# A hybrid decoder layer on one core: y of three head groups turned by VectorE and a round trip through memory instead of by TensorE

## The reference

```python
hn = rms_norm(h, norm_mix_w)
u, z, xbc, dt = split(hn @ w_in)                   # 512 | 1536 | 2560 | 24
y_pool = pool_mixer(u, pool_w, pool_scale)
xbc = silu(causal_dwconv(xbc, conv_w, conv_b))     # x 1536 | B 4x128 | C 4x128
y = ssd_chunked(x, softplus(dt + dt_bias), a, B, C) + d_skip * x   # 4 groups of 6 heads, chunks of 128
y = y * silu(z)
y = y * rsqrt(mean(y * y) + EPS) * ssm_norm_w      # mean over the 384 channels of a group
h = h + concat(y_pool, y) @ w_out
h = h + relu(rms_norm(h, norm_ffn_w) @ w_ff1) ** 2 @ w_ff2
out = rms_norm(h, norm_f_w)[:, N_META:]
```

## Time and profile before

| | us |
|---|---|
| median of 3 runs | 2657.96 (2656.44 to 2659.02) |
| profiled execution, its own time | 2655.4 |
| its span | 2653.7 |
| mixer steps of block 1 | from 452 to 652 |
| TensorE busy | 2630.8 (99% of the span) |

### The profile page before, as it was taken

One profiled execution on the slowest core, in us unless ns is written; L12 is line 12 of the kernel. 1 busy time (PEld: TensorE's weight loads), 2 busy tenths in 40 slices (PEclk: granted clock), 3 DMA queues, 4 the chain that ended last, 5 costly groups with the idle time before them and its releaser, 6 DMA issues.

```text
span 2653.7 us, 37407 instructions
## 1 busy us (share of the span) xinstructions
PE 2630.8 (99%) x13818; PEld 2199.1 (83%) x13818; DVE 1674.7 (63%) x2264; ACT 1241.4 (47%) x2474; POOL 1110.9 (42%) x866
## 2 busy tenths in 40 slices
PE   8999999999999999999999999999999999999998
PEld 6888788888888888888888888888888888888887
DVE  6788715888157882478853576564445766666667
ACT  4667653666236662356724455554544222222223
POOL 2133440345004450034544688665555435353434
PEclk9999999999999999999999999999999999999999
DMA  9977676886548866579773655764446742423324
GB/s 333 306 258 244 236 250 247 242 244 220 215 184 264 245 193 235 198 228 253 215 273 138 212 203 198 265 246 142 164 138 236 282 152 101 159 96 127 119 95 159
DMA packets 372739, 551.58 MB, mean 208 GB/s; under 512 B 139450, under 2 KB 240830, under 8 KB 364494
## 3 DMA queue, kind: packets, MB, share of 16 engines
q1 hardware_dynamic: 353550, 539.75, 60.1%
q10 hardware_dynamic: 19008, 9.44, 1.2%
HBM read 393.75 MB, written 155.39 MB: 207 GB/s over the span
## 4 chain that ended last, share of the span: by engine, by line
PE 52%; DVE 1%; DMA 1%; issue 1%; ACT 0%; POOL 0%; SPq 0%; POOLq 0%; ACTq 0%; DVEq 0%
PE bank L2337 22%; PE bank L2305 22%; PE bank L2031 3%; PE bank L1924 3%; PE bank L2011 1%; DMA pair_raw<-T_scr 1%; DVE stage L2812 0%; PE bank L2116 0%; PE bank L2134 0%; PE bank L2096 0%; DVE T_lo L2829 0%; PE bank L2084 0%; PE bank L2104 0%; PE bank L2050 0%; DVE T_lo L2819 0%
## 5 line engine op out<-in xcount | busy, mean ns | idle before, releaser
L1924 PE MATMUL bank<-hnT_hi,w_ring 128*128 128x512 f32 x1152 | 367.6, 391 | 1.6 <-ACT acc L1413 1.6
L2337 PE MATMUL bank<-w_first,T_hi 128*128 128x512 f32 x896 | 275.8, 389 | 0.0
L1924 PEld LDWEIGHTS bank<-hnT_hi,w_ring 128*128 128x128 f32 x1152 | 216.2, 188 | 47.6 <-ACT acc L1413 2.6
L2467 DVE SCALAR_TENSOR_TENSOR acc<-pre,par,acc 128x512 f32<-128x512 f32 x240 | 203.1, 846 | 79.2 <-ACT pre L1428 73.5
L2847 DVE TENSOR_TENSOR acc_th<-bank,acc_th 128x512 f32<-128x512 f32 x224 | 149.9, 685 | 154.1 <-PE bank L2337 153.2
L2305 PE MATMUL bank<-T_hi,w_both 128*128 128x512 f32 x768 | 242.5, 389 | 0.5 <-DVE ff L2788 0.5
L2031 PE MATMUL bank<-w_ring,T_hi 128*128 128x512 f32 x768 | 238.7, 392 | 0.0
L1924 PE MATMUL bank<-hnT_lo,w_ring 128*128 128x512 f32 x576 | 224.5, 390 | 0.0
L2337 PEld LDWEIGHTS bank<-w_first,T_hi 128*128 128x128 f32 x896 | 168.2, 188 | 34.9
L2011 PE MATMUL bank<-w_ring,hnT_hi 128*128 128x384 f32 x768 | 195.9, 335 | 0.6 <-DMA w_ring<-w_scr 0.6
L1924 PE MATMUL bank<-hnT_hi,w_both 128*128 128x512 f32 x544 | 181.9, 405 | 0.2 <-ACT pre L1428 0.2
(11 more groups left out here) (320 smaller groups left out, 6243.1 us busy)
## 6 DMA issues: line engine op xcount, KB each, us to landing
w_ring<-w_scr SPq DMA_DIRECT2D x312, 512.0 KB, 4.7
T_scr<-stage SPq DMA_DIRECT2D x32, 1792.0 KB, 6.6
w_scr<-w_both SPq DMA_DIRECT2D x100, 512.0 KB, 4.3
pair_raw<-in_w_ff SPq DMA_DIRECT2D x36, 1024.0 KB, 5.5
third<-T_scr SPq DMA_DIRECT2D x28, 1024.0 KB, 4.9
pair_raw<-T_scr SPq DMA_DIRECT2D x28, 1024.0 KB, 4.8
sums<-sums_scr SPq DMA_DIRECT2D x64, 384.0 KB, 5.3
raw<-in_w_in SPq DMA_DIRECT2D x36, 512.0 KB, 6.4
```

What stands on the lines that cost most here:

```text
L1924: mm = nc.tensor.matmul(bank[s][:, :], w[:, k, :], t[:, k, :], start=(k == 0 and j == 0), stop=(k == KT - 1 and j == 2))
L2337: mm = nc.tensor.matmul(bank[4 * half + t][:, :], a[:, k, tok], w[:, k, :], start=(SECOND[q % 7] not in GOES_ON and k == 0 and j == 0), st ...
L2467: ins = nc.vector.scalar_tensor_tensor(acc[:, s, 0:TB], pre[:, s, k:k + TB], w, acc[:, s, 0:TB], ALU.mult, ALU.add)
```

## The change

In blocks 1 to 3, for the twelve steps of groups 0 to 2, TensorE no longer turns y. VectorE turns its 32x32 squares into `y_turn` after `yo` of the next step; per group SyncE stores it (one DMA of 768 KB) and loads it back in four DMAs of 128-byte pieces to `y_raw`; ScalarE rounds the group in one instruction of 128x1536 and VectorE subtracts in one. This is done in steps 9 and 13 and behind the mixer. The load waits for its store on SyncE's queue. y of group 3 stays as it was.

x and B of the next group are no longer turned in `finish`, but four in a row in VectorE's step 3, after `yo` and the turn of y. ScalarE issues their four stores in a row in step 4, after the copy-out of z1 and before it rounds C, each after a wait for its turn. The state sum comes before `y_finish` in a step. The four tiles of h are stored at weight loads 16 (two), 24 and 32. At loads 24 and 32, SyncE stores y of a group, then h, then waits for y's store and loads y back, then loads tokens; y of group 2 goes at load 38.

```diff
 def store_turned (ScalarE)
-    def store_turned(b, v):
-        n = unit_of(b, v) if b and v >= ITEMS_G else None
-        if n is None or n >= U_POOL or n % UNITS_G not in (0, 2, 3, 4):
-            return
-        g, j = divmod(n, UNITS_G)
+    def store_turned(b, g, k):
+        j = TURNED[k]                                  # (0, 2, 3, 4)
+        x_turned.wait(act, b, len(TURNED) * (g - 1) + k + 1)
         act.dma_start(xt_scr[b, g, :, j - 2 if j else 3].rearrange("c p n -> p c n"),
...
@@ ScalarE, mixer
                             evac(b, n1)
                             tanh(b, pending)
+                            if b and c == CH - 1:
+                                for k in range(len(TURNED)):
+                                    store_turned(b, g + 1, k)
                         if b:
                             yoff_ps.wait(act, b, q)
...
-                        if q > 1:
+                        if q > 1 and turned_by_pe(b, q - 2):
                             y_high(b, q - 2)
+                        if b and q in (9, 13):
+                            y_group_high(b, q // CH - 2)
...
@@ VectorE, finish
-                        dst = group_tile(g, 0) if j == 0 else pre[:, s, 0:TB]
-                        steps.link(nc.vector.scalar_tensor_tensor(dst, ...))
-                        ...
-                        nc.vector.transpose(turn_tile(g, j), dst).then_inc(up_out.sem, 1)
@@ VectorE, mixer
+                        if b and q:
+                            state_add(b, q - 1)
                         if q:
                             y_finish(b, q - 1)
+                        if b == 0 and q:
                             state_add(b, q - 1)
...
-                        if q > 1 and (b or n1 is not None):
+                        if q > 1 and (q - 2 >= LAST_GROUP if b else n1 is not None):
                             y_low(b, q - 2)
                         if b:
                             xw_low(b, q)
...
                                                 ).then_inc(yo_ready.sem, 1)
+                        if b and 1 <= q <= LAST_GROUP:
+                            y_turning(b, q - 1)
+                        if b and n1 is not None and c == CH - 2:
+                            for k in range(len(TURNED)):
+                                x_turning(b, g + 1, k)
                         if n1 is None and c >= 2:
                             finish(b, pending - 1)
+                        if b and q in (9, 13):
+                            y_group_low(b, q // CH - 2)
...
+                def y_turning(b, q):
+                    g, c = divmod(q, CH)
+                    yn_ready.wait(dve, b, q + 1)
+                    if q == CH:
+                        hT_stored.wait(dve, b - 1, 128)
+                    if q == 2 * CH:
+                        hT_stored.wait(dve, b - 1, 192)
+                    nc.vector.transpose(y_turn[:, 3 * g:3 * g + 3, c, :],
+                                        y[:, :].rearrange("p (i f) -> p i f", f=P)
+                                        ).then_inc(y_turned.sem, 1)
...
@@ SyncE, weight loads
+                        if b and n in (3 * UNITS_G, 4 * UNITS_G):
+                            store_y(b, n // UNITS_G - 3)
+                        if b and n in H_STORED_AT:         # {16: (0, 2), 24: (2, 3), 32: (3, 4)}
+                            ...
+                        if b and n in (3 * UNITS_G, 4 * UNITS_G):
+                            load_y(b, n // UNITS_G - 3)
                         if b and g >= 2 and j == 0:
                             load_tokens(b, g - 1, 0)
```

More of the change, by code:

```diff
@@ L858, in load_tokens, with store_y, load_y @@
                             ).then_inc(xt_loaded[pair].sem, 16)
+                def store_y(b, g):
+                    y_turned.wait(sp, b, CH * (g + 1))
+                    sp.dma_start(y_scr[b, g].rearrange("i c p f -> p (i c) f"),
+                                 y_turn[:, 3 * g:3 * g + 3, :, :].rearrange("p i c f -> p (i c) f")
+                                 ).then_inc(y_stored.sem, 16)
+                def load_y(b, g):
+                    y_stored.wait(sp, b, 16 * (g + 1))
+                    blocks = y_scr[b, g].rearrange("i c (s a) (j f) -> j a (i c s) f", a=32, f=32)
+                    for j in range(4):
+                        sp.dma_start(y_raw[32 * j:32 * j + 32, 3 * g:3 * g + 3, :].rearrange(
+                            "p i (c f) -> p (i c) f", f=32), blocks[j]
+                            ).then_inc(y_back.sem, 16)
                 def load_quarter(i):
@@ L900, in _ @@
                                 load_sums(b, done, after)
-                        if b and n == 24:
-                            hT_stored.wait(sp, b - 1, 128)
-                        if b and n in (16, 24):
-                            for t in (0, 1) if n == 16 else (2, 3):
+                        if b and n in (3 * UNITS_G, 4 * UNITS_G):
+                            store_y(b, n // UNITS_G - 3)
+                        if b and n in H_STORED_AT:
+                            first, after = H_STORED_AT[n]
+                            if first:
+                                hT_stored.wait(sp, b - 1, 64 * first)
+                            for t in range(first, after):
                                 store_turned_h(b - 1, t)
+                        if b and n in (3 * UNITS_G, 4 * UNITS_G):
+                            load_y(b, n // UNITS_G - 3)
                         if b and g >= 2 and j == 0:
@@ L2254, in _ @@
                                 pool_lo.wait(pe, b, 4)
+                            if b and d == 0 and u in (0, 3):
+                                y_group_lo.wait(pe, b, 2 + u // 3)
                             if d == 0 and u == 6:
-                                yT_lo.wait(pe, b, STEPS)
+                                yT_lo.wait(pe, b, CH if b else STEPS)
                             if d == 0:
@@ L2555, in y_finish @@
                     ty_ready.wait(dve, b, q + 1)
-                    yT_ps.wait(dve, b, q)
+                    if b and 0 < q <= LAST_GROUP:
+                        y_turned.wait(dve, b, q)
+                    else:
+                        yT_ps.wait(dve, b, pe_turn(b, q) if q else 0)
                     ssy_ready.wait(dve, b, q)
```

102 lines of the change are left out of this document (68 added, 34 removed).

## The result

Slower, and by more than the range held: 2695.94 us (2692.74 to 2697.08, four runs) against 2657.25 (2656.44 to 2659.02, four runs), a ratio of 1.0143, 95% interval 1.0125 to 1.016. The profiled execution of the changed kernel spans 2694.4 us.

The account below looks back on a forecast made before the run. TensorE, balanced to 0.1 us with a chain over the other engines, was taken as the bound. 1.9 + 1.3 + 2.1 - 0.45 = 4.9 us a block, 14.6 in three, gave 2672.6 us; range 2647 to 2684.

Parts of the forecast that it names:

- The state sum first ... so VectorE starts 0.5 later: VectorE ahead of `yo`: the state sum waits for TensorE's state product, 0.5 us in group 1, 0.75 and 0.7 in group 0.
- rival 3: TensorE's clock falls to the 1.2 GHz level after waits of 2 to 3 us; 2678 to 2700 us; chance 0.1.
- the last needs the last turn ... The issue takes 0.37, the signal some 0.05.: ScalarE, step 4: C follows the last store's issue; the exponential ends 3.65 us behind the last turn.
- The split of y in group 2: 2.1 us.: Group 2, step 2: splitting group 0's y takes VectorE 1.76 us; TensorE goes on 2.1 us later.
- TensorE's transposes: 0.42 us a step.: Three transposes cost TensorE 0.42 us a step, 15.1 us over 36 steps.
- So the group is balanced to 0.1 us ... a saving on TensorE is worth only what that chain gains too.: At B in group 1, TensorE and the chain over other engines match within 0.1 us; both must gain.
- DMA at nothing: 2048 more small pieces, 2.8 us by rate, costed at nothing as covered; otherwise 0 to 3 us a block.
- Rivals 1 and 2: ScalarE's stores cost nothing: 2640 to 2650 us, chance 0.2; chain 1.5 us less late per group: 2653 to 2663, chance 0.12.
- rival 4: Late weights through the full DMA queue, +15 plus 3 to 9 us: 2675 to 2684; chance 0.06.

Follow-up runs that it names:

- state last: The changed kernel with the state sum behind `y_finish` as before, nothing else: 2686.32 us, ratio 1.0108.
- stores behind the falls: The changed kernel with ScalarE's four stores of step 4 issued behind the six falls of E, not ahead of C rounded: 2676.06 us, ratio 1.0069.
- y's way: The changed kernel with x and B turned in `finish` and the state sum behind `y_finish`, both as before: 2666.2 us, ratio 1.0033.
- Behind the squares: The changed kernel with ScalarE's four stores of step 4 issued behind the squares of y: 2683.69 us, ratio 1.0101.

## Why the prediction was wrong

The direction and the place were right: C rounded behind the four issues, the exponential late, B waiting six times for the copy-out of z2. The size was not; 4.9 us a block stood for 14.5, 13.5 and 9.9. The table shows where it grew. `yo`, B and the group's end are counted from the first C·S product of their group and set against the same mark of the kernel before; plus is later. The three values are blocks 1 to 3, in us.

| | `yo` of step 3 | C behind the last turn | B | added from B to the group's end |
|---|---|---|---|---|
| group 0, forecast | -0.75 | 0.45 | +1.9 | 0 |
| group 0, changed | -0.35, -0.36, -0.35 | 2.32, 1.45, 0.49 | +3.97, +3.10, +2.15 | +1.97, +2.23, +1.28 |
| group 1, forecast | -1.3 | 0.45 | +1.3 | 0 |
| group 1, changed | +0.45, +0.40, +0.40 | 0.86, 0.77, 0.95 | +3.28, +3.16, +3.32 | +1.05, +1.26, -0.31 |
| group 1, state last | -1.86, -1.86, -1.87 | 1.62, 2.15, 1.95 | +1.72, +2.27, +2.05 | +1.35, +1.06, +1.24 |

The three blocks took 23.3 us more than the sum had for them. B's start in groups 0 and 1 has 9.4 of these, what follows B there 7.5, group 2 has 5.2 and group 3 1.3. Step by step:

- **"The state sum first ... so VectorE starts 0.5 later"**, and 0.75 and 0.7 in group 0. This term failed most. The sum for `yo` of group 1 was -2.7 + 1.0 - 0.1 + 0.5 = -1.3; measured +0.4. With the state sum back in its place it is -1.86, which is the same sum without the 0.5. So the order cost 2.3 us there and not 0.5, and 2.0 in group 0 where the sum had 1.45. It is also what group 2 took beyond the forecast: state last takes 2.4, 1.7 and 1.8 us away there. The state sum of step 4 in group 1, foretold half a microsecond earlier, came 0.9 to 1.0 later. I priced the waiting, and took each VectorE duration from rows in which it happened to be short; in another phase to GpSimd `xw` is 1.18 and not 0.55, a tap 1.4 and not 0.75. In time the order is worth 17 us by itself, 9.6 in the changed kernel and 20 where x and B are turned in finish.
- **The clock**, which the sum put at nothing (rival 3, chance 0.1), came true beside the forecast, not in place of it: some 8 us, the 7.5 behind B. My waits of 2 to 3 us were 2.6 to 4.8, and the rows showed only that 0.6 us is safe and 7.2 is not. Without it the time would have been 2688, still outside the range.
- **"the last needs the last turn ... The issue takes 0.37, the signal some 0.05."** The path was right, the size was not: issues in a row took up to 1.75 us each. C came 0.5 to 2.3 us behind the last turn in group 0 and 0.8 to 0.95 in group 1 for the 0.45 of the forecast, which is 4.1 us in the six places. That moving the stores behind the falls gave 20 us is the price of their place, part of which the sum had charged.
- **The split of y in group 2: 2.1 us.** Measured 4.4, 3.6 and 3.5 for the group, but 2.0, 1.9 and 1.7 with the state last. So the term came out about right, though VectorE's split took 2.30 for 1.76.
- **TensorE's transposes: 0.42 us a step.** Measured 0.31, where nothing waits: 11.2 us in all. The distance to the next instruction's start isn't what its absence saves.
- **"So the group is balanced to 0.1 us ... a saving on TensorE is worth only what that chain gains too."** Half right. With two of three transposes gone, groups 1 and 2 kept about half of the saving; group 0 gained more than all of it, by VectorE's shorter products. My sum charged all of the removed transposes as lost in waits.
- **DMA at nothing.** Right for TensorE's weights in the changed kernel, and wrong once the faults above it were removed: then tokens come late behind y's load (8.1 us of ScalarE's waiting).
- Rivals 1 and 2 asked for a chain no longer than before; rival 4, late weights, doesn't show in the waits after.

The parts don't add up. By themselves x and B in a row cost 26 us, the state sum's place 17 and y's way 9: 52, for 39 together.

What stays open: how much of the 17 us the longer instructions are; why an issue takes 0.37 us at one time and 1.75 at another; and whether y's round trip can be made without hurting a load.

## What to carry to other kernels

When every engine's list closes into a loop, a swap of two instructions can cost more than the work that a change moves: make each part of a change by itself first. Price an instruction by its range over the trace and not by one row, above all VectorE's and GpSimd's, which lengthen each other. A DMA issue on a compute engine is an instruction of that engine with all that follows queued behind it, and a round trip through memory has to be priced in the queue that issues it.

## What the runs showed of the hardware

- ScalarE's 36 issues of a 128x512 store took 0.37 to 0.74 us each by themselves (kernel before) and 0.37 to 1.75 in a row (changed). Behind the squares, where the turns were done before the first issue, they still took up to 1.75. In the changed kernel one took 1.69 beside SyncE's issues (625.5 us) and one 1.38 with none under way (857.8).
- Of the 126 taps of 128x512 between the first and the 13th C·S product of blocks 1 to 3, before the change, 27 started while a GpSimd instruction was under way and took 1.37 to 1.44 us; the other 99 took 0.73 to 0.75. With the state sum first 42 started so, and took 1.37 to 1.40.
- Behind waits of TensorE of 2.01 (stores behind the falls, block 2), 2.74, 3.14 and 4.84 us the granted clock of the next 3.6 us was 0.63, 0.53, 0.50 and 0.50, and behind others of 2.72, 3.12 and 3.49 (state last, block 3) it was 1.00: the length of the wait alone doesn't tell.
- 18 needless transposes in the wait, 2.1 us of them, left waits of 0.6 to 2.2 us behind them and kept the clock at 1.00 each time.
- Three transposes between a unit and the diagonal product cost 0.31 us by their absence and 0.42 by their starts; two of the three, 0.19 and 0.22.
